# Scores held with turned sign, the fused minimum used as the exponential's bias, and row sums taken from columns of ones in the output product

## The reference, cut to what matters

```python
# first block: 4 "fox" heads, 4 "moba" heads, 4 "swa" heads (band of 128 keys, with a sink)
s = einsum('qd,kd->qk', q, k) * HEAD_DIM ** -0.5 + bias      # masked places get -1e30
p = softmax(s)                     # swa: one more column, the sink, which takes weight and has no value
o = einsum('qk,kd->qd', p, v)
# second block: 8 heads, each with a branch "slc" and a branch "win" over the causal keys
o_h = gate_slc * attend(q_h, k_slc, v_slc) + gate_win * attend(q_h, k_win, v_win) + gate_cmp * o_cmp
```

## Time and profile before

| what | value |
|---|---|
| median of 3 runs | 1075.43 us (1075.04 to 1077.15) |
| span of the profiled execution, first to last instruction | 1074.8 us |
| mean granted TensorE clock | 0.983 of full |
| PE busy | 997.8 us, 93% of the span |
| DVE, ACT, POOL busy | 423.5, 397.5, 391.0 us |
| chain that ended last | PE 81%, DVE 11%, issue 3%, ACT 2%, POOL 2% |

### The profile page before, as it was taken

The page is one execution under the profiler, slowest core; times in us unless marked ns, Lnnn a source line. Parts: engine busy times, 40 slices in busy tenths (PEclk is TensorE's granted clock), DMA queues, the critical chain, the costliest instruction groups (busy, mean ns, idle before and its releaser), DMA issues.

```text
span 1074.8 us, 13360 instructions
## 1 busy us (share of the span) xinstructions
PE 997.8 (93%) x5055; PEld 817.6 (76%) x5055; DVE 423.5 (39%) x1012; ACT 397.5 (37%) x832; POOL 391.0 (36%) x314
## 2 busy tenths in 40 slices
PE   6979999999998999989988889699999999999995
PEld 3867677777876887878877788578888888888884
DVE  3462632348655444437468653440000000122224
ACT  4232333343845224233555444333222222333332
POOL 4461422234221524222320003644444454454443
PEclk9989999999998999999999999899999999999998
DMA  6652121121115331052130002133232323232311
GB/s 224 195 180 48 42 77 40 40 79 64 40 41 196 98 137 61 22 176 79 58 119 1 2 1 79 40 106 110 80 116 78 118 79 118 79 118 79 111 46 79
DMA packets 68064, 92.82 MB, mean 86 GB/s; under 512 B 9740, under 2 KB 47153, under 8 KB 68000
## 3 DMA queue, kind: packets, MB, share of 16 engines
q1 hardware_dynamic: 68000, 91.97, 26.4%
HBM read 89.82 MB, written 6.85 MB: 90 GB/s over the span
## 4 chain that ended last, share of the span: by engine, by line
PE 81%; DVE 11%; issue 3%; ACT 2%; POOL 2%; DMA 0%; SPq 0%; DVEq 0%; ACTq 0%
PE psum L999 62%; PE psum L1240 4%; PE psum L1200 4%; PE psum L1215 2%; DVE prob L1822 2%; PE psum L1073 1%; PE psum L1292 1%; POOL st L2085 1%; PE psum L1168 1%; PE psum L1268 1%; DVE sq L1725 1%; ACT prob L1507 1%; PE psum L1253 1%; PE psum L1036 1%; PE psum L1282 1%
## 5 line engine op out<-in xcount | busy, mean ns | idle before, releaser
L2057 POOL TENSOR_TENSOR WR<-RAW,WR 128x512 fp32r<-128x512 f32 (+2 forms) x268 | 341.5, 1283 | 586.2 <-ACT WR L1379 586.2
L999 PE MATMUL psum<-WR,XT 128*128 128x512 f32 (+2 forms) x2160 | 501.6, 388 | 7.0 <-DVE st L736 3.8
L999 PEld LDWEIGHTS psum<-WR,XT 128*128 128x128 f32 x2160 | 390.8, 190 | 83.1 <-DVE st L736 4.2
L1379 ACT ACTIVATE WR<-RAW 128x512 fp32r<-128x512 f32 (+2 forms) x268 | 161.3, 615 | 263.3 <-PE psum L999 251.0
L999 PE MATMUL psum<-XT,WR 128*128 128x512 f32 x1056 | 240.5, 390 | 1.5 <-issue 1.5
L999 PEld LDWEIGHTS psum<-XT,WR 128*128 128x128 f32 x1056 | 198.0, 188 | 42.5 <-issue 1.7
L1507 ACT ACTIVATE prob<-prob,st 128x512 f32<-128x512 f32 (+2 forms) x112 | 61.2, 547 | 162.6 <-DVE st L1831 149.1
L1678 DVE TENSOR_TENSOR actT<-psum,gated 128x512 f32<-128x512 f32 x22 | 14.2, 686 | 203.4 <-ACT gated L1459 203.4
L1240 PE MATMUL psum<-V,probT 128*128 128x128 f32 x536 | 78.3, 288 | 14.1 <-DVE R L1855 8.5
L1240 PEld LDWEIGHTS psum<-V,probT 128*128 128x128 f32 x536 | 69.5, 198 | 22.8 <-issue 14.1
L2014 DVE TENSOR_TENSOR XT<-actT,XT 128x512 fp32r<-128x512 f32 x22 | 28.4, 1290 | 84.6 <-ACT XT L1563 84.6
(11 more groups left out here) (209 smaller groups left out, 790.7 us busy)
## 6 DMA issues: line engine op xcount, KB each, us to landing
RAW<-in_w_gate_up_dram SPq DMA_DIRECT2D x44, 512.0 KB, 4.3
RAW<-in_w_in_dram SPq DMA_DIRECT2D x16, 1024.0 KB, 5.4
RAW<-in_w_down_dram SPq DMA_DIRECT2D x11, 1024.0 KB, 4.8
RAW<-in_w_out_dram SPq DMA_DIRECT2D x8, 1024.0 KB, 5.0
RAW<-in_w_in_dram SPq DMA_DIRECT2D x12, 512.0 KB, 4.2
rep_scratch<-rows_scratch SPq DMA_DIRECT2D x12, 320.0 KB, 7.3
R<-in_x_dram SPq DMA_DIRECT2D x4, 512.0 KB, 5.7
x_again<-in_x_dram SPq DMA_DIRECT2D x1, 2048.0 KB, 7.8
```

The source lines that it names most:

```text
L999: last = pe.matmul(outp, stationary(x), moving(y), start=start and n == 0, stop=stop and n == 2)
L1379: act.activation(WR[:, s % RING, 0, 0:w], RAW[:, g % 2, q, 0:w], ACT.Copy).then_inc(w_hi, 1)
L2057: pool.tensor_tensor(WR[:, s % RING, 1, 0:w], RAW[:, g % 2, q, 0:w], WR[:, s % RING, 0, 0:w].bitcast(F32), ALU.subtract).then_inc(w_lo, 1)
```

## The change

It does five things, in 28 heads with 80 S groups:

1. The scores carry the opposite sign: the gains on q, the keys `kS`, the bias rows, `fox_c` and the causal mask are turned, each in an instruction that was there already.
2. The fused instruction takes the minimum instead of the maximum and writes it straight to `nm`, the exponential's bias; the exponential has scale -1. In the 72 groups that are not swa, the wait (`link`) and the small sign instruction fall away. In the 8 swa groups they stay, for the sink.
3. The exponential no longer sums into its accumulator.
4. The product with V reads 64 columns of ones and 64 columns of V in place of two heads' V: still 128 columns. The result lies in the order of row blocks (`i`), ones first, so each row block's sum stands in PSUM beside its output.
5. The reciprocal (for swa the addition before it) reads the four sums from PSUM. For fox, moba and swa one `tensor_tensor` with a broadcast factor scales all 4 blocks; slc and win keep their 4 instructions.

```diff
+        ones_up = at("ones_up", ONES_AT, [2 * (V_AT + NT * 896)])
+        V1 = ones_up[:, V_AT:V_AT + NT * 896].rearrange("p (t n) -> p t n", t=NT)
...
+        def ones_and_v(name, h, j):
+
+            words = V_AT
+            if name in ("slc", "win"):
+                at_ = words + 2 * P * j + (0 if name == "slc" else P) + HD * (h // 4)
+            elif name == "swa":
+                at_ = words + 896 * j + 768 + HD * (h // 2)
+            else:
+                at_ = words + 896 * j + 256 * KINDS1[name] + HD * h
+            return ones_up[:, 0:2 * at_].rearrange("p (x n) -> p x n", x=2)[:, :, 0:HD]
...
-                            last = pe.matmul(OB[:, P * n:P * n + P], probT[:, at_:at_ + P], v_of(name, h, j + b)[0],
-                                             start=b == 0, stop=b == m - 1)
+                            last = pe.matmul(OB[:, P * i:P * i + P].rearrange("p (x n) -> p x n", x=2), probT[:, at_:at_ + P],
+                                             ones_and_v(name, h, j + b), start=b == 0, stop=b == m - 1)
...
                         last = act.activation(buf[:, col:col + m * P], buf[:, col:col + m * P], ACT.Exp,
-                                              bias=nm[:, sl + n:sl + n + 1], accum_out=sm[:, sl + n:sl + n + 1])
+                                              bias=nm[:, sl + n:sl + n + 1], scale=-1.0)
...
+            dve.memset(ones_up[:, 0:HD], 1.0)
...
+                dve.tensor_scalar(minus_sinks, minus_sinks, -1.0, None, ALU.mult)
...
-                dve.tensor_copy(fox_c[:, h, :], SC[nth[step] % 2]).then_inc(sc_out, 1)
+                dve.tensor_scalar(fox_c[:, h, :], SC[nth[step] % 2], -1.0, None, ALU.mult).then_inc(sc_out, 1)
...
                         last = dve.tensor_tensor_reduce(buf[:, col:col + m * P], SC[nth[step] % 2][:, col:col + m * P],
-                                                        bias_of(name, h, i, m), 1.0, -3e38, ALU.add, ALU.max,
-                                                        mx[:, sl + n:sl + n + 1])
-                    link(last)
-                    ns = slice(sl + first_n, sl + n + 1)
+                                                        bias_of(name, h, i, m), 1.0, 3e38, ALU.add, ALU.min,
+                                                        nm[:, sl + n:sl + n + 1])
                     if name == "swa":
 
-                        dve.tensor_scalar(nm[:, ns], mx[:, ns], sinks[:, h:h + 1], -1.0, ALU.max, ALU.mult).then_inc(sc_out, 1)
-                    else:
-                        dve.tensor_scalar(nm[:, ns], mx[:, ns], -1.0, None, ALU.mult).then_inc(sc_out, 1)
+                        link(last)
+                        ns = slice(sl + first_n, sl + n + 1)
+                        last = dve.tensor_scalar(nm[:, ns], nm[:, ns], minus_sinks[:, h:h + 1], None, ALU.min)
+                    last.then_inc(sc_out, 1)
...
+                    parts = OB.rearrange("p (i x d) -> p i x d", i=NT, x=2)
+                    sums = parts[:, :, 0, 0]
                     if name == "swa":
-                        link(dve.tensor_tensor(sm[:, sl:sl + 4], sm[:, sl:sl + 4], es[:, sl:sl + 4], ALU.add))
-                    link(dve.reciprocal(ri[:, sl:sl + 4], sm[:, sl:sl + 4]))
+                        link(dve.tensor_tensor(ri[:, sl:sl + 4], sums, es[:, sl:sl + 4], ALU.add))
+                        sums = ri[:, sl:sl + 4]
+                    link(dve.reciprocal(ri[:, sl:sl + 4], sums))
...
+                    else:
+                        lo = 256 * KINDS1[name] + HD * h
+                        last = dve.tensor_tensor(R2[:, :, lo:lo + HD], parts[:, :, 1, :],
+                                                 ri[:, sl:sl + 4].unsqueeze(2).broadcast_to([P, NT, HD]), ALU.mult)
                     last.then_inc(o_out, 1)
```

More of the change, by code:

```diff
@@ L98, in constants @@
         "suffix": np.ascontiguousarray(tri.T),
-        "causal": np.where(i[None, :] > i[:, None], np.float32(MASK), np.float32(0)),
+        "causal": np.where(i[None, :] > i[:, None], np.float32(-MASK), np.float32(0)),
         "strict": np.where(i[:, None] >= i[None, :], np.float32(MASK), np.float32(0)),
@@ L501, in hybrid_two_block_kernel @@
         b_forget = st[:, 50:54]
-        sinks = st[:, 54:58]
+        minus_sinks = st[:, 54:58]
         ss = st[:, 58:62]
@@ L519, in hybrid_two_block_kernel @@
         cf8 = st[:, 418:450]
-        tab1 = st[:, 450:458]
-        tab2 = st[:, 458:466]
-        negmu = st[:, 466:470]
-        ss_g = st[:, 474:478]
-        rr_g = st[:, 478:482]
-        ss_a = st[:, 470:474]
+        tab1 = st[:, 162:170]
+        tab2 = st[:, 170:178]
+        negmu = st[:, 130:134]
+        ss_g = st[:, 138:142]
+        rr_g = st[:, 142:146]
+        ss_a = st[:, 134:138]
         psum = ctx.enter_context(nc.psum_tensor("psum", [P, 8, 512], F32))
@@ L769, in evacuate @@
                     yield copy(V2[:, t, 1, :], m[:, 128:256])
-                    yield copy(g_tmp.rearrange("p (c q) -> p c q", q=4)[:, :, POS[t]], m[:, 256:280])
+                    yield copy(g_tmp.rearrange("p (c q) -> p c q", q=4)[:, :, t], m[:, 256:280])
                 elif ch == 3:
@@ L877, in small_loads @@
                 bcast(b_forget, a["b_forget"], 4).then_inc(s_const, 16)
-                bcast(sinks, a["sinks"], 4).then_inc(s_const, 16)
+                bcast(minus_sinks, a["sinks"], 4).then_inc(s_const, 16)
             def store_rows():
@@ L1507, in _ @@
                         last = act.activation(buf[:, col:col + m * P], buf[:, col:col + m * P], ACT.Exp,
-                                              bias=nm[:, sl + n:sl + n + 1], accum_out=sm[:, sl + n:sl + n + 1])
+                                              bias=nm[:, sl + n:sl + n + 1], scale=-1.0)
                         if name == "swa":
-                            last = act.activation(es[:, sl + n:sl + n + 1], nm[:, sl + n:sl + n + 1], ACT.Exp, bias=sinks[:, h:h + 1])
+                            last = act.activation(es[:, sl + i:sl + i + 1], minus_sinks[:, h:h + 1], ACT.Exp,
+                                                  bias=nm[:, sl + n:sl + n + 1], scale=-1.0)
                     last.then_inc(e_done, 1)
@@ L1587, in setup @@
                 dve.tensor_copy(strict[:, :], stage[:, 128:256])
+                dve.tensor_scalar(minus_sinks, minus_sinks, -1.0, None, ALU.mult)
                 for n in range(3):
-                    last = dve.tensor_scalar(qk_gain[:, 2 * n:2 * n + 1], qk_gain[:, 2 * n:2 * n + 1], QSCALE, None, ALU.mult)
+                    last = dve.tensor_scalar(qk_gain[:, 2 * n:2 * n + 1], qk_gain[:, 2 * n:2 * n + 1], -QSCALE, None, ALU.mult)
                 last.then_inc(setup_dve, 1)
@@ L1599, in _ @@
                         dve.wait_ge(tab_done, n + 1)
-                        dve.tensor_copy(rows[0:8, lo:hi], bank[0:8, 0:hi - lo]).then_inc(tab_out, 1)
+                        dve.tensor_scalar(rows[0:8, lo:hi], bank[0:8, 0:hi - lo], -1.0, None, ALU.mult).then_inc(tab_out, 1)
                 if step == ("ev", "in1", 0):
@@ L1771, in _ @@
                         v = kS[0 if name == "slc" else 1][:, :, :, tok]
-                        last = dve.tensor_tensor(v[:, 1], TR[:, 0:256].rearrange("p (g n) -> p g n", g=2), v[:, 0].bitcast(F32), ALU.subtract)
+                        last = dve.scalar_tensor_tensor(out=v[:, 1], in0=TR[:, 0:256].rearrange("p (g n) -> p g n", g=2), scalar=-1.0,
+                                                        in1=v[:, 0].bitcast(F32), op0=ALU.mult, op1=ALU.subtract)
                     last.then_inc(tr_out, 1)
@@ L1847, in _ @@
                         link(dve.tensor_tensor(ri[:, sl:sl + 4], ri[:, sl:sl + 4], gates[:, gc:gc + 4], ALU.mult))
-                    for gg in range(len(plan)):
-                        for i, j, m, col, n in segments(plan, gg):
-                            at_ = P * n + HD * v_of(name, h, 0)[1]
-                            src = OB[:, at_:at_ + HD]
-                            f = ri[:, sl + n:sl + n + 1]
-                            if name in ("slc", "win"):
-                                dst = R1[:, i, HD * h:HD * h + HD]
-                                last = dve.scalar_tensor_tensor(out=dst, in0=src, scalar=f, in1=dst, op0=ALU.mult, op1=ALU.add)
-                            else:
-                                lo = 256 * KINDS1[name] + HD * h
-                                last = dve.tensor_scalar(R2[:, i, lo:lo + HD], src, f, None, ALU.mult)
+                        for i in range(NT):
+                            dst = R1[:, i, HD * h:HD * h + HD]
+                            last = dve.scalar_tensor_tensor(out=dst, in0=parts[:, i, 1, :], scalar=ri[:, sl + i:sl + i + 1], in1=dst,
+                                                            op0=ALU.mult, op1=ALU.add)
+                    else:
+                        lo = 256 * KINDS1[name] + HD * h
+                        last = dve.tensor_tensor(R2[:, :, lo:lo + HD], parts[:, :, 1, :],
```

(1 more changed line is left out.)

14 lines of the change are left out of this document (6 added, 8 removed).

## The result

The changed kernel takes 1070.47 us (median of 6 runs, 1064.2 to 1073.17), the kernel before beside it 1076.64 (6 runs, 1075.04 to 1077.97): 0.9938 of the time before, 95% interval 0.9913 to 0.9964. That is 6.2 us faster, and 0.4 us from the forecast of 1070.1. The forecast was counted from the 1075.4 of three earlier runs; counted from the 1076.64 it would have been 1071.3, so a part of this nearness is luck. The profiled execution took 1068.46 us.

A forecast was written before the change was run, and what follows sets the result against it. PE bounds the kernel (81% of the chain), so only its pauses ended by softmax work can shrink: 1.0 + 1.6 + 0.8 + 1.0 + 0.9 = 5.3 us, 1075.4 - 5.3 = 1070.1 us; range 1067.5 to 1073.5.

The forecast's parts named there:

- Kinds 1 to 3: O behind the scaling in slc and win 1.0 us, T behind the exponential 1.6, pauses around the input transposes 0.8.
- the pair at 611 and 615: Pauses of 1.79 and 2.07 us with the input transposes, ending a VectorE and ScalarE chain: together 0.8 us gained.
- five of them stand just before a wait of kind 1, which takes the gain back: Of seven short T waits for the exponential, 0.27 us each, all vanish but only two count: 0.5 us.
- kind 1: O behind the scaling in slc and win: seven waits gain 0.14 us each, 1.0 us.
- The 0.58 before 570.67: T's 0.80 us wait for the exponential: two signs and two accumulator reads leave its chain, gaining 0.58 us.
- the longest T wait: T's 1.2 us wait behind the exponential: one sign and three accumulator reads leave its chain, gaining about 0.5 us.
- Kind 4: The two swa waits of O behind the scaling: 0.59 us before the longer, 0.39 before the other, together 1.0 us.
- Kind 5: T behind layout copies sharing bank TR: the sign ahead of the copy goes, seven waits give 0.9 us.
- slower: Rival: the product with ones costs more per matmul; from 0.014 us each the kernel is over 0.2% slower; chance 0.06.
- Nothing is won: Rival: all these pauses are set by PE's own round trip, which takes up the slack: 1075 us; chance 0.06.
- Passed on: Rival: earlier T or O finds another engine; T and input-transpose waits gain half or less: 1072.5 us; chance 0.17.
- The rival of the clock: Rival: shorter pauses at 611 and 615 also remove the slow clock stretch at 616, 1.6 us: 1068.5 us; chance 0.17.

The follow-up runs named there:

- experiment 3: Changed kernel with four 64-column scaling instructions again in fox, moba and swa heads: 1072.84 us, ratio 0.996 to the kernel before.
- experiment 2: Changed kernel with the exponential summing again into columns nobody reads, so its 112 accumulator reads are back: 1070.94 us, ratio 0.9951 to the kernel before.
- Experiment 1: Changed kernel with a wait and small VectorE copy put back in the 72 groups that are not swa: 1076.77 us, ratio 0.9996 to the kernel before.
- experiment 7: Kernel before with the turned sign alone, minimum straight into the bias; sums, product and scalings as they were: 1073.82 us, ratio 0.998.
- experiments 4 and 8: Changed kernel, one 256-column multiplication releasing the output bank: 4 in slc and win, 1070.49 us; 8 in win only, ahead of the gate, 1068.05 us.
- second pair: Both kernels run once more, unaltered, on one chip: the changed kernel 1070.97 us, ratio 0.9948; the kernel before 1075.87 us beside 1076.44.
- the last experiment: Changed kernel with the output bank released by one 256-column multiplication before the gate in window heads 3 to 7 only: 1066.72 us, ratio 0.9908.
- 9 and 10: Changed kernel with one more VectorE operation ahead of window head 3's transposed copy: 9 with 512 columns, 1072.49 us; 10 with 256, 1071.4 us.

## Why the prediction held, point by point

**Kinds 1 to 3: near in sum, wrong in place.** The prediction put 1.0 us on O behind the scaling, 1.6 on T behind the exponential and 0.8 on the pair at 611 and 615, 3.4 in all. The view's rows give 0.2 on O (8.5 to 8.3, not 7.5), 2.5 on T behind the exponential (3.9 to 1.4) and 0.7 on T behind VectorE's copy (1.8 to 1.1), which is 3.4 again, but only because it drops what is left of T's waits. In full they give 0.36, 1.90 and 0.67: 2.9. Two steps failed. The first is "five of them stand just before a wait of kind 1, which takes the gain back". It was the other way about: in the last heads the wait for the exponential went from 0.23 to 0.10 and the O wait from 0.57 only to 0.50. The second is that a wait of T with no wait of kind 1 behind it was counted in full. The 0.58 before 570.67 did come, 0.80 to 0.21, but the next O, which had hardly waited (the T ends at 570.67 + 0.63, the S matmuls between end at 571.76, the O starts at 571.85), now waits 0.42 for the scaling:

```profile
571.85 1.13 PE L1240 MATMUL psum<-V,probT 128*128 128x128 f32 x8
```

```profile
564.51 0.63 PE L1226 MATMUL psum<-ident_sb,prob 128*128 128x128 f32 x4 [0.21 <-ACT prob L1518]
...
566.02 1.13 PE L1251 MATMUL psum<-ones_up,probT 128*128 128x128 f32 x8 [0.42 <-DVE R L1867]
```

That is also why the view's first line counts 8 waits, where it had 7. And the longest T wait, which was to lose some 0.5, lost 0.2 (1.16 to 0.96). The head's distance fell by 0.17, with 0.14 predicted, so the queue's row of VectorE was priced rightly; the reciprocal's PSUM read costs 0.01 (177 ns, against 170 in the same 24 heads before) and not 0.05, which is most of the 0.03 between them. The pair was nearly right: 0.68 was predicted for the first pause and it fell from 1.79 to 1.12, 0.28 less 0.05 for the second and it fell from 2.07 to 1.79 (the earlier trace rows against these two). Of this the T behind them, which waited 0.10 and now waits 0.26 (611.52), took 0.16 back.

```profile
603.97 0.66 PE L1226 MATMUL psum<-ident_sb,prob 128*128 128x128 f32 x4 [1.12 <-DVE probT L812]
...
607.33 1.13 PE L1251 MATMUL psum<-ones_up,probT 128*128 128x128 f32 x8 [1.79 <-DVE R L1867]
```

**Kind 4, swa: 1.3 instead of 1.0.** The terms that were mis-sized: the single scaling gave 1.0 (experiment 3; 0.88 predicted) and the accumulator reads 0.4 (experiment 2; 0.20 predicted). The price of one read was right and their number was not. The prediction counted the two reads ahead of the last `xt` copy; two more stand ahead of the `xt` copy before it, and VectorE's next fused adds stand in its queue behind what that copy releases:

```profile
326.24 1.05 ACT L1392 ACTIVATE XT<-psum 128x512 fp32r<-128x512 f32 x2
...
331.08 1.05 ACT L1392 ACTIVATE XT<-psum 128x512 fp32r<-128x512 f32 x2
```

From the one to the other it is 4.84 us before and with the sums back (326.69 and 331.53), and 4.66 in the changed kernel (323.21 and 327.87): 0.18 for two reads. The text of experiment 2, on record before its run, has all four, 0.4 us, and 0.37 came.

**Kind 5: right.** 3.0 to 2.0 us in the view, 0.91 in full, 0.9 predicted, and in its parts too: four of the seven waits fell by 0.18 or 0.19, two by 0.08 or 0.09, one (210.08, with its T at 211.59) not at all. Experiment 1 brought it back and experiment 7 had it alone.

**Not in the sum: 0.5 us** in full, 0.3 on T behind ScalarE's copy and 0.2 behind the transposed `ws`. Together 2.9 + 1.3 + 0.9 + 0.5 = 5.6, where 5.3 was forecast: 0.5 too much in kinds 1 to 3, 0.3 too little in swa, 0.5 left out.

**The rivals.** The product with ones costs nothing (285 and 288 ns), so "slower" is out. "Nothing is won" is out by the earlier trace rows against their counterpart. "Passed on" happened in two places of the change, 0.33 us from T to the O behind 570.67 and 0.16 to the T behind the pair, and not in the bulk of it; experiments 4 and 8 show that this kernel does more of it as soon as VectorE's work grows. The rival of the clock was right in its first half: the stretch at 616 is gone and 1.6 us with it, and the one in swa, which I said would stay, was halved. It was wrong in its second, that this comes off the time: the clock takes 1.7 to 3.1 us back behind 644 us. By what the prediction wrote (wrong "if the granted clock falls at another place than at 334, 557 and 615 us") this point failed, and the number held because gain and loss of the clock nearly cancel, which is luck. In the second pair: 5.65 of pauses, 1.6 at 615 and 0.9 in swa (2.2 in the table less 1.3 of pauses), less 3.1 between the blocks, is 5.05; the traces differ by 5.5 from 76 us on. 0.4 us are not accounted for.

**Open.** Why the stretch between the blocks is 10.2, 13.7 or 17.1 us long. The kernel before (twice), the sign alone, the sums back and the last experiment had 10.2; the changed one had 13.7 and 17.1, experiment 3 13.7, and experiments 1, 4, 8, 9 and 10 17.1. The time of arrival doesn't sort them: PE's matmuls of experiments 2 and 3 reach 644 us within 0.13 us of each other, and they had 10.2 and 13.7. The kernel's own part in it can't be told from chance with one or two executions of each.

## What to carry to other kernels

Price an instruction that is removed from an engine's queue by its place ahead of each wait, and look at the next wait of the same round trip, also at one too short to be listed: it can take the gain over. Sum the pauses with the short ones in, and trust the sum more than the split between neighbouring lines. Test the parts one by one, and compare the pauses as well as the times; here pauses add up to 0.1 us while times are over 3 us off, and only the traces with the clock's record tell why. Where an engine both frees a buffer and works on, put the release as early as it can stand, and only there where the work that this delays isn't waited for.

## What the runs showed of the hardware

- Between 76 and 644 us the half-rate stretches of TensorE's granted clock came at the same places, with the same lengths, in two executions of each of two kernels. Behind the pause of some 10 us between the blocks the length differed between two executions of the changed kernel (13.7 and 17.1 us), 1.5 us of time.
- Where two pauses some 3.6 us apart shrank from 1.79 and 2.07 us to 1.12 and 1.79, such a stretch behind them was gone, and 1.6 us with it; that their length was the cause is not shown.
- The instruction behind a fused instruction starts in the same instant as the read of its accumulator (630.64 both), also when it is an ordinary reciprocal.
- A VectorE reciprocal of 4 columns takes 177 ns out of PSUM and 170 out of SBUF in the same 24 heads. The four of swa, out of SBUF in both kernels, take 178, so the source is not all that sets it.
- Each read of ScalarE's accumulator behind an exponential took 0.09 to 0.10 us of its queue (4.84 against 4.66 us for two).
- A matmul whose 128 moving columns are 64 and 64, some 20 KB and more apart in each partition, lasts as long as one over 128 neighbouring columns (eight of them 1.13 us, either way).
